# The starts of on-chip tensors moved within 512 bytes: weights, activations and attention outputs set apart

## The reference

```python
x = x + 0.5 * rms_norm(swiglu_ffn(rms_norm(x, norm_pre[l, 0]), ffn1_w_in[l], ffn1_w_out[l]), norm_post[l, 0])
mixed = token_mixer(rms_norm(x, norm_pre[l, 1]), ...)
x = x + rms_norm(mixed, norm_post[l, 1])
x = x + 0.5 * rms_norm(swiglu_ffn(...ffn2...), norm_post[l, 2])
...
for layer in range(2):
    x = layer_norm(alpha * x + mix, ...)
    x = layer_norm(alpha * x + cross_attend(x, mem, xa_wq, xa_wkv, xa_wo), ...)
    x = layer_norm(alpha * x + conv_ffn(x, ffn_w_up, ffn_conv_w, ffn_conv_b, ffn_w_down), ...)
```

## Time and profile before

| | |
|---|---|
| median of 3 runs | 2421.17 us (2420.96 to 2421.32) |
| profiled execution | 2421.15 us |
| its span, first to last instruction | 2419.4 us |
| mean granted TensorE clock | 0.996 |
| instructions | 27040 |
| matmuls busy | 2396.1 us, 99% |
| VectorE, ScalarE busy | 1092.4 us, 806.9 us |
| read from memory | 234.46 MB, 98 GB/s over the span |

### The profile page before, as it was taken

One profiled execution on the slowest core, in us unless ns is written; L12 is line 12 of the kernel. 1 busy time (PEld: TensorE's weight loads), 2 busy tenths in 40 slices (PEclk: granted clock), 3 DMA queues, 4 the chain that ended last, 5 costly groups with the idle time before them and its releaser, 6 DMA issues.

```text
span 2419.4 us, 27040 instructions
## 1 busy us (share of the span) xinstructions
PE 2396.1 (99%) x12164; PEld 2034.0 (84%) x12164; DVE 1092.4 (45%) x1036; ACT 806.9 (33%) x891; POOL 65.1 (3%) x39
## 2 busy tenths in 40 slices
PE   9999999999999999999999999999999999999998
PEld 8888889888888888898987888888888977888887
DVE  4333225565553332255735644423535546544424
ACT  4232224454542232233432433321322432433311
POOL 0000000230100000000000000000000000000000
PEclk9999999999999999999999999999999999999999
DMA  4232323211133232242421322321422511232321
GB/s 162 87 105 90 120 87 120 79 38 70 48 110 105 87 105 98 85 162 88 159 85 35 122 104 88 105 105 70 157 93 82 192 70 70 88 105 88 121 94 63
DMA packets 34405, 238.30 MB, mean 98 GB/s; under 512 B 3949, under 2 KB 4333, under 8 KB 6514
## 3 DMA queue, kind: packets, MB, share of 16 engines
q1 hardware_dynamic: 34288, 236.56, 27.3%
q10 hardware_dynamic: 2, 0.00, 0.0%
HBM read 234.46 MB, written 2.10 MB: 98 GB/s over the span
## 4 chain that ended last, share of the span: by engine, by line
PE 97%; ACT 1%; DVE 1%; DMA 1%; issue 0%
PE bank L444 54%; PE bank L518 28%; PE bank L850 4%; PE bank L483 4%; PE bank L506 1%; PE bank L877 1%; PE bank L704 1%; PE bank L897 1%; DMA raw<-w_full 1%; PE bank L636 0%; ACT w_hi L1020 0%; PE bank L646 0%; PE bank L587 0%; PE bank L605 0%; PE bank L888 0%
## 5 line engine op out<-in xcount | busy, mean ns | idle before, releaser
L444 PE MATMUL bank<-a_hi,w_hi 128*128 128x512 f32 (+1 forms) x2112 | 785.5, 372 | 0.6 <-DVE a_lo L1546 0.6
L444 PE MATMUL bank<-a_lo,w_hi 128*128 128x512 f32 (+1 forms) x2112 | 781.0, 370 | 0.0
L444 PE MATMUL bank<-a_hi,w_lo 128*128 128x512 f32 (+1 forms) x2112 | 781.0, 370 | 0.0
L1497 DVE TENSOR_TENSOR w_lo<-raw,w_hi 128x2048 fp32r<-128x2048 f32 x207 | 476.4, 2302 | 504.3 <-ACT w_hi L1020 503.4
L1020 ACT ACTIVATE w_hi<-raw 128x2048 fp32r<-128x2048 f32 x207 | 394.4, 1906 | 367.5 <-DMA raw<-w_full 367.5
L444 PEld LDWEIGHTS bank<-a_hi,w_hi 128*128 128x128 f32 x2112 | 398.0, 188 | 69.7 <-issue 1.7
L444 PEld LDWEIGHTS bank<-a_lo,w_hi 128*128 128x128 f32 x2112 | 397.9, 188 | 67.7
L444 PEld LDWEIGHTS bank<-a_hi,w_lo 128*128 128x128 f32 x2112 | 398.1, 188 | 67.5 <-issue 0.7
L518 PE MATMUL bank<-w_hi,h_hi 128*128 128x512 f32 x704 | 274.5, 390 | 0.2 <-DVE w_lo L1497 0.2
L518 PE MATMUL bank<-w_hi,h_lo 128*128 128x512 f32 x704 | 274.0, 389 | 0.0
L518 PE MATMUL bank<-w_lo,h_hi 128*128 128x512 f32 x704 | 273.9, 389 | 0.0
(11 more groups left out here) (284 smaller groups left out, 2317.1 us busy)
## 6 DMA issues: line engine op xcount, KB each, us to landing
raw<-w_full SPq DMA_DIRECT2D x207, 1024.0 KB, 4.7
rows_ab<-rows SPq DMA_DIRECT2D x8, 1024.0 KB, 5.3
x<-x SPq DMA_DIRECT2D x4, 512.0 KB, 5.7
mem_raw<-mem SPq DMA_DIRECT2D x2, 1024.0 KB, 8.2
out<-x SPq DMA_DIRECT2D x4, 512.0 KB, 2.6
raw<-w_full SPq DMA_DIRECT2D x2, 512.0 KB, 5.7
ab_rows<-ab_rows SPq DMA_DIRECT2D x1, 768.0 KB, 7.6
wg_raw<-w_gates SPq DMA_DIRECT2D x1, 512.0 KB, 5.8
```

What stands on the lines that cost most here:

```text
L444: last = mm(bank[:, b + m, cols], w[:, s, c0:c0 + P], act_in[:, k, cols], start=(k == 0 and j == 0), stop=(k == KD - 1 and j == 2))
L1497: V.tensor_tensor(w_lo[:, u % SLOTS, :], raw[:, u % SLOTS, :], w_hi[:, u % SLOTS, :], ALU.subtract).then_inc(w_split, 1)
```

## The change

The tensors keep their shapes, their order and their uses. Only where they begin changes. The activations `a_hi` and `a_lo` begin 128 bytes later. `raw`, `w_lo`, `w_hi`, and all that stands behind them (`ident`, `ones`, `vec`, `small`, `stat`, `bnl`, `tri`) begin 256 bytes later, and so does `row0`, which lies over `w_hi`. `o_hi` and `o_lo` in the arena begin 256 bytes earlier. The rest of the arena and `x` stay.

```diff
-        a_hi = at("a_hi", [P, KD, T], f32r, X0 + 16 * KB)
-        a_lo = at("a_lo", [P, KD, T], f32r, X0 + 32 * KB)
-
-        raw = at("raw", [P, SLOTS, FULL], f32, X0 + 48 * KB)
-        w_lo = at("w_lo", [P, SLOTS, FULL], f32r, X0 + 48 * KB)
-        w_hi = at("w_hi", [P, SLOTS, FULL], f32r, X0 + 80 * KB)
-        C0 = X0 + 112 * KB
+
+        a_hi = at("a_hi", [P, KD, T], f32r, X0 + 16 * KB + 128)
+        a_lo = at("a_lo", [P, KD, T], f32r, X0 + 32 * KB + 128)
+        W0 = X0 + 48 * KB + 256
+
+        raw = at("raw", [P, SLOTS, FULL], f32, W0)
+        w_lo = at("w_lo", [P, SLOTS, FULL], f32r, W0)
+        w_hi = at("w_hi", [P, SLOTS, FULL], f32r, W0 + 32 * KB)
+        C0 = W0 + 64 * KB
...
-        row0 = at("row0", [1, D], f32, X0 + 80 * KB)
+        row0 = at("row0", [1, D], f32, W0 + 32 * KB)
...
-        o_hi = arena("o_hi", [P, KD, T], f32r, 48)
-        o_lo = arena("o_lo", [P, KD, T], f32r, 64)
+        o_hi = arena("o_hi", [P, KD, T], f32r, 47.75)
+        o_lo = arena("o_lo", [P, KD, T], f32r, 63.75)
```

## The result

The changed kernel takes 2450.81 us (median of 4 runs, 2449.21 to 2453.01) against 2421.07 us (2419.53 to 2421.32): ratio 1.0125, 95% interval 1.0107 to 1.0142. It is 29.7 us slower. The forecast of no change was wrong, and the range, which ended at 2446, ended 5 us too early.

A forecast was written before the change was run, and what follows sets the result against it. The prediction took the number of TensorE matmuls by their spacing to bound the kernel. 2421.2 us plus 10584 x 0, 0 for fp32 and at most 0.1 for VectorE and ScalarE gave 2421.2 us, range 2408 to 2446.

The forecast's parts named there:

- The forecast of no change: Whole kernel: distance between operands has no effect, time 2421.2 us, chance 0.69.
- What bounds the kernel: TensorE: time is the number of matmuls by their spacing; matmuls on for 2396.1 of 2419.4 us.
- 13.3 ns surplus: Split matmuls: spacing beyond streaming time, alike for 512 and 256 columns; 146 us over 10968 matmuls.
- The counts by distance: Split matmuls sorted by distance of weights to activations after the change; 10584 of 10968 get a new distance.
- The price of a distance: Extra time per moved split matmul: taken as 0, bounded by 12.1 ns less and 13.3 ns more.
- looks like a fixed step between two matmuls: Reason for price 0: the same 13.3 ns, 32 periods, over both widths, both weight roles and every pair of names.
- Plain fp32 as a witness: L955, L667, L897: about 0.43 us at every distance, suggesting no effect; doubted because fp32 has a tenth of the surplus.
- Distance 256 and o at 0: Weights 256 past h, m, y and mem, 3264 matmuls, priced 0; weights and o, 384, unmoved at distance 0.
- The slower rival: Load and stream disturb each other off distance 0: 4.7 ns per matmul, 50 us, 2471 us; chance 0.17.
- if only the 128 distance is bad: Variant of slower: 7296 matmuls by 4.7 ns, 34 us, giving 2455 us; within the chance of 0.17.
- The faster rival: Distance 0 itself costs; off it the load hides as in fp32: 128 us less, 2293 us; chance 0.14.
- Identity, tri, VectorE, ScalarE and the loads: Other moved operands and transfers: counted 0 us, with 0.1 us at most for VectorE and ScalarE.

The follow-up runs named there:

- e9: Kernel before with only mem_hi, mem_lo and k_mem 64 bytes up: 2417.24 us against 2420.09, ratio 0.9989.
- e2: Kernel before with weights and all behind them 256 bytes up, nothing else moved, every pair at distance 256: 2420.67 us, ratio 1.0001.
- e1: Kernel before with a 384 up, weights and all behind them 512 up, so only weights to a is 128: 2450.97 us, ratio 1.0131.
- e8: Kernel before with a 64 up, weights and all from C0 96 up, o 64 down, giving distances 32, 96 and 160: 2469.68 us, one run.
- e11: Kernel before with every tensor 64 bytes up, all distances unchanged: 2419.18 us in one run.
- e6: Kernel before with raw and w_lo 128 bytes up, w_hi, row0 and C0 512 up: 2448.97 us in one run.
- e10: Kernel before with a_lo 128 bytes up, weights and C0 512 up, so only a_lo is at 128: 2439.90 us in one run.
- e3: Kernel before with weights and all behind them 128 bytes up, nothing else moved, every pair at distance 128: 2465.17 us, ratio 1.0189.

## Why the prediction was wrong

- What bounds the kernel: right. The time is the matmuls by their spacing, and the whole loss is in TensorE's busy time. That the 13.3 ns surplus was the only place an address could touch was right too.
- The counts by distance: right, and they carried the result: 7296 at 128 (with the 24 of L605, 7320), 3264 at 256, 384 at 0.
- The price of a distance: wrong. The step that failed is "the value I take is 0", with its reason that the surplus "looks like a fixed step between two matmuls" and that a stream passes every position within 512 bytes anyway. It is no fixed step: the surplus over the streaming time, 13.3 ns before, measured 19.1 to 20.0 ns for wide ones at 128, 20.0 at 32, 96 and 192, 15.6 in most stretches at 64, and 6.7 in some for narrow ones at 64. In this change that put 6.0 ns on each of the 5376 wide matmuls at 128, where the prediction had 0. That the surplus was equal over widths, roles and names was no evidence, because in the kernel before every one of these pairs stood at distance 0; that equality held the one quantity fixed that the change moved. The two tensors' distance was the same in all 10968 rows, so the rows could not speak on it.
- Plain fp32 as a witness: misleading. Its spacing does not depend on the distance, but that of the split matmuls does. The record of L877 stays at 379 ns with k_mem 64 past q_at (e9); the change itself moves no pair of L877 or L897 apart, so their equal records after it say nothing. The prediction named this doubt and gave it too little weight.
- Distance 256 and o at 0: priced at nothing, and nothing it was (e2).
- The slower rival: its form "if only the 128 distance is bad" gave 2455 against 2450.8. Its price, 4.7 ns from the earlier trace rows, was small by a fifth for wide matmuls (6.0) and wrong in sign for narrow ones (-1.2), two errors of 7 and 11 us, opposite in sign, so that 34 us came out only 4 too high, by luck. It deserved more than a part of 0.17: the earlier trace rows was the one place where these matmuls showed that their spacing can change.
- The faster rival: a load that hides as in fp32 was seen at no distance for wide matmuls. For narrow ones half of it exists, 113.4 ns.
- Identity, tri, VectorE, ScalarE and the loads: 0, and so measured; VectorE's and ScalarE's busy times differ by 0.2 us.

The Trainium skill (TensorE: Matmul & The Clock Gate, "Back-to-back issue gap") has 518 cycles, 215.8 ns, from one warm 512-column matmul to the next; no stretch of wide split matmuls here came below 226.7. The 32 cycles that the Trainium skill gives there, as theory, for a block of weights ("Weight-path perf modes") match the surplus of 13.3 ns at distances 0 and 256, but not the wide one at any other, so they do not fix it.

What stays open: why the stream's start against a stationary block matters modulo 256 bytes. Many of the means differ by 6.6 to 6.7 ns, 16 periods of 2.4 GHz, though 232.4 and 234.3 do not fit. That would suit a load and a stream that take turns at something they share, but no run shows that thing. Also open is what decides into which pattern a stage settles.

## What to carry to other kernels

Where spacing of matmuls sets the time, compute the start of each stream against its stationary block, and keep it at a multiple of 256 bytes for 512 columns; for a tensor that only meets streams of 256 columns, 64 bytes off was better here, by 3 us of 2420. A constant that is the same in all rows of a trace may be constant because the trace holds its cause fixed: before calling it a property of the chip, ask whether any row varies what the change varies. Here a disturbed stretch of the very same instructions was a better witness for the price than a calm one of another type.

## What the runs showed of the hardware

- Split (float32r) matmuls with a weight load each were 226.7 ns apart for 512 columns where stream and stationary block began at equal places modulo 256 bytes, and 228.9 to 234.3 where not (e1 to e8); for 256 columns 113.4 (in stretches at 64 and 192) to 119.9. The absolute place did not count (e11).
- A stream was slowed by its distance to its own stationary block and by that to the one that loads under it (e6, e10: records 6 to 8 ns longer either way), and with both off the mean was 232.4 ns, not twice the surcharge (e3).
- With a_lo alone at 128 the same program settled into 228.8, 231.1 or 233.3 ns for a whole stage, and differently in another execution; its times spread by 9 us. At distance 0 and 256 this was not seen: every long stretch has 226.7.
- Plain fp32 matmuls showed none of it (L877 at 379 ns with its operands 64 bytes apart, e9).
